# Second block of a two-block model: 32-wide products in the heads' inverse, and another order of the second input projection

## The chip, the core and the metric

The kernel runs on one core of a Trainium2 chip, as one launch. The metric is the device time in microseconds. Five engines work beside each other: PE (TensorE) multiplies matrices, with its weight loads (PEld) overlapping; DVE (VectorE), ACT (ScalarE) and POOL (GpSimd) work element by element; SP issues DMAs. They meet at semaphores only.

## The reference

Two blocks, one behind the other, on 256 tokens of 1024 channels, all in float32. The first is a mixer with a mixture of 32 experts; the second, where nearly all of the change lies, is cut here to its core:

```python
h = _rmsnorm(x, norm_mix_g)
proj = h @ w_in                       # 1024 x 7168: r, k, v | glu_in | gate logits
rkv = rkv + (_token_shift(rkv) - rkv) * mu_rkv
# low-rank products on h + dh * mu_lora[j], dh = shift(h) - h
w_log = -softplus(-(w0 + tanh(xw @ w1) @ w2)) - 0.5;  a = sigmoid(a0 + (xa @ a1) @ a2)
g = sigmoid(xg @ g1) @ g2
# per head (16 heads of 64), over 256 steps:
S = S * w_t + (S @ -kk_t) (kk_t * a_t)^T + v_t k_t^T ;  o_t = S @ r_t
o = group_norm(o) * ln_g + ln_b + bonus;  a_out = o * g
u = glu_in[:1024] * sigmoid(glu_in[1024:])      # then a causal convolution, 31 taps per channel
c_out = silu(layer_norm(conv(u)))
x = x + (gates0 * (a_out @ w_rwkv) + gates1 * (c_out @ w_conv)) @ w_out
x = x + square(relu(h2 @ w_ff1)) @ w_ff2
```

## The kernel before

The 256 tokens stand as two tiles (`NT = 2`) of 128 partitions. Dense weights come in quarters of 128x1024 by SP's DMAs into a ring of four (`RING = 4`). Each is split: ACT writes the high part `whi` (line 301), POOL or DVE the rest `wlo` (line 306), and PE does 12 products per quarter: 4 of line 326, 4 of 327, then, once `wlo` is there, 4 of 330. Each engine's order is written out by hand, function by function, and a wait names a semaphore and a count.

**The second input** (`pe_in2`, `act_in2`, `dve_in2`). 14 tiles of 512 columns, p = 0 to 13, four quarters each, in the order `TILES2`. Two PSUM banks take one tile, the next two the next, so tile p waits until tile p - 2 has been read out.

- p = 0 to 3 are the gated input of the convolution. ACT copies or sigmoids each tile out of PSUM (line 2269), and `gate_glu(j)` on DVE multiplies the halves (line 2352). PE then turns the result by transposes (`turn_u`, line 2183) and DVE copies it to `uT` (`copy_u`, line 2393).
- The low-rank products (lines 2204 and 2206, then 2218) need `lora_in` less `lora_lerp`: DVE multiplies the weights by mu (line 2382), subtracts (2385), and scales `hT` (2387).
- `convolve` on DVE is 31 rounds for each of two sets of four chunks, so 62 rounds of 4 instructions (lines 2411 and 2414), accumulating in PSUM. They are dealt out between DVE's other work by `CONV_FIRST` and `CONV_NEXT`.
- p = 4 to 9 are r, k, v. `shift_out` scales two products of each tile (lines 2330, 2335), ACT moves the result down one token by three DMAs (2281 to 2283), and `shift_in` adds (2344). PE's tile p + 2 waits for it.
- p = 10 to 13 are the gates, with a bias product of one row (line 2167) ahead of each. Behind tile 11 come `cs`, a cumulative sum for the first pair of heads (line 2232), then `pe_conv_back`, which transposes the convolution's result (line 2450) and waits for it and for `pdiff`, a DVE difference (line 2510) made from `cs`.

**The heads** (`pe_heads`, `act_heads`, `dve_heads`). 16 heads are worked as 8 pairs, p = 0 to 7, one `step` each; steps 1 to 6 are a loop, and steps 0 and 7 have parts of the dense products between their pieces. A pair is four units (2 heads, 2 token tiles), each with a triangular 128x128 matrix whose inverse is built by doubling over 7 levels. At a level, PE makes `below` (line 2672), DVE masks it (`mask`, line 3105), PE makes `grow` (lines 2686 and 2691), and ACT copies halves of it back (`grown`, lines 2918 and 2919). At levels 0 to 5 these are products of 64x64 on the two diagonal halves (`HALF`), which sit on two separate quarters of PE's array. Between `below` and `grow` PE has a piece of the pair before (`rest`, `solve`, `state`, `outputs`, products over 128 partitions) or of the next (`turn_ar`, `turn_bk`, `grams`). `begin_inverse` on DVE makes the level-0 operands: one pass (line 3089) and two masks (3093) for each two units.

**The experts.** `pe_scatter` adds a group's result to the tokens by four products (line 1743) into banks 3, 6, 7, 3; the fourth waits until DVE has added the first (line 1751).

## Time and profile before

| | |
|---|---|
| median of 3 runs | 1346.9 us (1345.45 to 1347.27) |
| the profiled execution | 1349.64 us, of it the span 1347.7 us |
| PE busy in the span | 1289.7 us (96%) |
| DVE / ACT / POOL busy | 848.8 (63%) / 724.2 (54%) / 571.8 us (42%) |
| granted TensorE clock, mean | 0.978 |

The times of all rows come from the one profiled execution, from the start of its span. The second input stands at about 682 to 929 us, the heads at 929 to 1100 us. PE's busy time is modelled from pipelined matmuls, so 96% does not say that it works at its peak: a stretch is judged by what ended the idle time and by how densely instructions start. PE does a float32 product as two instructions in the trace: a line that the code's order shows as x4 has x8 in the timeline.

### The profile page before, as it was taken

What the parts mean: (1) busy time and instruction counts of PE and PEld (TensorE: products, weight loads), DVE (VectorE), ACT (ScalarE), POOL (GpSimd) and SP (SyncE); (2) the same over time, 40 slices, a digit from 0 to 9 for tenths busy, and PEclk for the clock granted to TensorE, in tenths of its full rate; (3) what the DMA queues carried; (4) which work ended last, traced back from release to release, by engine and by line L of the source; (5) the groups of instructions that cost most, each with busy time, mean ns of one, the idle gap of its engine ahead of it and who ended that gap; (6) DMA issues with size and microseconds to landing.
All of it is one profiled execution on the core that took longest, in us unless ns stands there. A gap on an engine that the chain in (4) does not pass through costs nothing.

```text
span 1347.7 us, 22434 instructions
## 1 busy us (share of the span) xinstructions
PE 1289.7 (96%) x7929; PEld 1040.8 (77%) x7929; DVE 848.8 (63%) x1578; ACT 724.2 (54%) x1252; POOL 571.8 (42%) x252
## 2 busy tenths in 40 slices
PE   7999999897999999999999899899999999999997
PEld 6978878786887887877677677676888877788886
DVE  1576466547788888888568998854777763221213
ACT  5564666546666776766564133574433334554544
POOL 5886674350000000000489257645100017788884
PEclk9999999898899999999999898989999999999999
DMA  6665453267799999997476266633100006555552
GB/s 216 192 185 144 131 166 125 63 188 246 243 343 318 323 315 337 318 305 266 135 221 196 86 186 190 202 88 113 56 3 2 18 2 204 160 185 188 185 192 89
DMA packets 128515, 240.07 MB, mean 178 GB/s; under 512 B 16428, under 2 KB 23470, under 8 KB 128420
## 3 DMA queue, kind: packets, MB, share of 16 engines
q1 hardware_dynamic: 116656, 227.12, 52.8%
q10 hardware_dynamic: 11765, 11.67, 3.3%
q8 instruction: 62, 1.02, 0.3%
q14 instruction: 32, 0.26, 0.1%
HBM read 234.57 MB, written 1.05 MB: 175 GB/s over the span
## 4 chain that ended last, share of the span: by engine, by line
issue 44%; PE 24%; POOL 18%; DVE 10%; DMA 3%; ACT 1%; ACTq 1%; POOLq 0%; DVEq 0%
POOL wlo L306 18%; DVE bank L2414 4%; PE bank L326 3%; PE bank L330 3%; PE bank L327 3%; DMA work<-proj 2%; PE bank L2672 2%; PE bank L2686 2%; PE bank L2691 1%; PE bank L2648 1%; PE bank L2736 1%; PE bank L2716 1%; PE bank L2708 1%; PE bank L2737 0%; DVE proj L2344 0%
## 5 line engine op out<-in xcount | busy, mean ns | idle before, releaser
L306 POOL TENSOR_TENSOR wlo<-raw,whi 128x1024 fp32r<-128x1024 f32 (+1 forms) x232 | 560.9, 2437 | 619.9 <-ACT whi L301 615.4
L301 ACT ACTIVATE whi<-raw 128x1024 fp32r<-128x1024 f32 (+1 forms) x300 | 312.0, 1055 | 254.0 <-PE bank L330 130.1
L326 PE MATMUL bank<-whi,t0h 128*128 128x512 f32 (+1 forms) x552 | 226.3, 410 | 6.1 <-ACT whi L301 3.9
L327 PE MATMUL bank<-whi,t0l 128*128 128x512 f32 (+1 forms) x552 | 221.1, 401 | 0.0
L330 PE MATMUL bank<-wlo,t0h 128*128 128x512 f32 (+1 forms) x552 | 151.7, 397 | 1.6 <-POOL wlo L306 1.6
L326 PEld LDWEIGHTS bank<-whi,t0h 128*128 128x128 f32 x552 | 106.5, 193 | 37.8 <-issue 6.3
L330 PEld LDWEIGHTS bank<-wlo,t0h 128*128 128x128 f32 x552 | 105.8, 192 | 26.8 <-POOL wlo L306 2.9
L327 PEld LDWEIGHTS bank<-whi,t0l 128*128 128x128 f32 x552 | 106.6, 193 | 23.2 <-issue 1.0
L306 DVE TENSOR_TENSOR wlo<-work,whi 128x1024 fp32r<-128x1024 f32 x96 | 113.1, 1220 | 7.7 <-ACT whi L301 7.7
L1660 PE MATMUL bank<-whi,t0h 128*128 128x512 f32 x256 | 106.8, 417 | 0.0
L1661 PE MATMUL bank<-whi,t0l 128*128 128x512 f32 x256 | 102.2, 399 | 0.0
L301 ACT ACTIVATE whi<-work 128x1024 fp32r<-128x1024 f32 x96 | 98.3, 1059 | 3.7 <-PE bank L1687 3.7
L2414 DVE SCALAR_TENSOR_TENSOR bank<-work,proj,bank 128x256 f32<-128x256 f32 x232 | 96.4, 485 | 1.6
L306 DVE TENSOR_TENSOR wlo<-raw,whi 128x1024 fp32r<-128x1024 f32 x68 | 81.8, 1242 | 12.7 <-ACT whi L301 12.4
L3511 DVE TENSOR_TENSOR bank<-bank,work 128x256 f32<-128x256 f32 x32 | 13.4, 428 | 112.9 <-ACT work L3436 112.9
L1665 PE MATMUL bank<-wlo,t0h 128*128 128x512 f32 x256 | 81.8, 401 | 0.0
L3012 POOL TENSOR_TENSOR proj<-proj,small x8 | 4.9, 617 | 138.6 <-PE bank L2737 138.6
L1665 PEld LDWEIGHTS bank<-wlo,t0h 128*128 128x128 f32 x256 | 48.6, 191 | 12.8 <-DVE wlo L306 1.1
L1660 PEld LDWEIGHTS bank<-whi,t0h 128*128 128x128 f32 x256 | 49.3, 192 | 10.8 <-issue 0.7
L1661 PEld LDWEIGHTS bank<-whi,t0l 128*128 128x128 f32 x256 | 48.9, 191 | 10.7 <-issue 0.7
L2918 ACT COPY work<-bank 128x64 f32<-128x64 f32 x80 | 17.1, 214 | 68.2 <-PE bank L2691 62.4
L1761 ACT ACTIVATE t1h<-bank 128x256 fp32r<-128x256 f32 x32 | 12.4, 387 | 75.0 <-PE bank L1671 75.0
(528 smaller groups left out, 2514.2 us busy)
## 6 DMA issues: line engine op xcount, KB each, us to landing
raw<-in_w_in SPq DMA_DIRECT2D x96, 512.0 KB, 3.8
raw<-in_w_ff SPq DMA_DIRECT2D x64, 512.0 KB, 3.7
work<-in_w_exp_down SPq DMA_DIRECT2D x68, 256.0 KB, 6.0
work<-in_w_exp_gate SPq DMA_DIRECT2D x62, 256.0 KB, 5.9
work<-in_w_exp_up SPq DMA_DIRECT2D x62, 256.0 KB, 7.2
raw<-in_w_exp_down SPq DMA_DIRECT2D x60, 256.0 KB, 5.6
raw<-in_w_in SPq DMA_DIRECT2D x20, 464.0 KB, 4.2
raw<-in_w_exp_gate SPq DMA_DIRECT2D x34, 256.0 KB, 5.9
```

Source lines behind the costliest of these rows:

```text
L301: nc.scalar.activation(whi[:, s, 0:width], raw_of(n)[:, 0:width], ACT.Copy).then_inc(hi_ready, 1)
L306: ins = (nc.vector if split_by_vector(n) else nc.gpsimd).tensor_tensor(wlo[:, s, 0:width], raw_of(n)[:, 0:width], whi[:, s, 0:width].bitca ...
L326: nc.tensor.matmul(dst[t][:, 0:width], hi[:, k, r], wh[:, kk, :], start=k == 0 and not begun, stop=False)
L327: nc.tensor.matmul(dst[t][:, 0:width], lo[:, k, r], wh[:, kk, :], start=False, stop=False)
L330: mm = nc.tensor.matmul(dst[t][:, 0:width], hi[:, k, r], wl[:, kk, :], start=False, stop=k == KC - 1)
L1660: nc.tensor.matmul(dst, t0h[:, k, r], wh[:, :, kk, :], start=k == 0, stop=False)
L1661: nc.tensor.matmul(dst, t0l[:, k, r], wh[:, :, kk, :], start=False, stop=False)
L1665: mm = nc.tensor.matmul(dst, t0h[:, k, r], wl[:, :, kk, :], start=False, stop=k == KC - 1)
L2414: ins = nc.vector.scalar_tensor_tensor(out=cvT[:, c, :] if w == W2 - 1 else partial(c), in0=uT[:, c, w:w + SEQ], scalar=tap, in1=partial(c ...
L2672: mm = nc.tensor.matmul(o[r], gram[b][r, u, r], ident[r, r] if lev == 0 else Xm[r, u, :], start=True, stop=True)
L2686: nc.tensor.matmul(bank[2 + g][r, v * 64:(v + 1) * 64], XD[b][r, u, :], Ym[r, u, :], start=True, stop=True)
L2918: nc.scalar.copy(halves(Xm[:, r, :], lev)[0], halves(new[:, 0], lev)[0]).then_inc(xm_copied.sem, 1)
```

## The change

It has three parts.

1. **Inverse.** At levels 0 to 4 the blocks are at most 32 wide, so the products are made on the four diagonal 32x32 blocks (`BLOCK`, `SMALL = 5`) in place of the two 64x64 halves. Level 0 makes both operands by products with the identity, which `mask_first` masks in one pass, and the masks of line 3093 go. At level 4 ACT spreads the 32-wide result to 64 with zeros by four scaled copies for each two units in place of two copies. On DVE the preparation of the next pair is dealt out anew (`make_r`, `make_a`, `sum_bonus`, `squares`), and `centre` loses one instruction.
2. **Second input.** `TILES2` starts 8, 6, 9, 7: the sigmoid half of each gated pair comes first and the other is multiplied straight out of PSUM in `gate_glu`, so two of four evacuations go. The products by mu (`lerp`) are made by ACT. `turn_u(1)` moves inside tile 4, `cs` ahead of tile 11, `pdiff` ahead of the last six rounds of the convolution.
3. **Experts.** The fourth product of `pe_scatter` goes to bank 2, without the wait; the next block's use of bank 2 waits instead.

```diff
                     if q == 1:
+                        if added:
+                            pe.wait_ge(x_added, added)
                         turn_hidden(E, b)
...
-                if z == 3:
-                    pe.wait_ge(x_added, 4 * J - 3)
-                nc.tensor.matmul(bank[(3, 6, 7, 3)[z]][:, :], back[:, J - 1, t, :], ysum[:, 512 * h:512 * h + 512],
+                nc.tensor.matmul(bank[(3, 6, 7, 2)[z]][:, :], back[:, J - 1, t, :], ysum[:, 512 * h:512 * h + 512],
...
-        TILES2 = [6, 8, 7, 9] + list(range(6)) + list(range(10, 14))
+        TILES2 = [8, 6, 9, 7] + list(range(6)) + list(range(10, 14))
...
-        CONV_FIRST, CONV_NEXT = (12, 8, 4), (3, 2)
+        CONV_FIRST, CONV_NEXT, CONV_LAST = (10, 3, 7, 2), (3, 2), 4
-            return min(tiles, RKV2) + max(tiles - GATES2, 0)
+            return (min(tiles, RKV2) + 1) // 2 + max(tiles - GATES2, 0)
...
+                elif p in (3, 5):
+                    pe.wait_ge(*glu_ready.at(p - 1))
...
-            tile(4)
-            turn_u(1)
+            def second_chunks():
+                pe.wait_ge(*lora_act.at(3))
+                turn_u(1)
+
+            tile(4, second_chunks)
...
-            for p in range(9, 12):
-                tile(p)
-
+            tile(9)
+            tile(10)
             pe.wait_ge(*state_decay_ready.at(1))
             mm.then_inc(cs_done, 1)
+            tile(11)
...
+            def lerp(j):
+                c = (slice(0, 64), slice(64, P), slice(P, 2 * P))[j]
+                for k in range(KC):
+                    ins = nc.scalar.activation(lora_lerp[:, k, c], lora_in[:, k, c], ACT.Copy, scale=mul[:, j, k:k + 1])
+                ins.then_inc(lora_lerped, 1)
...
+            act.wait_ge(lora_in_loaded, 48)
+            lerp(0)
+            lerp(1)
...
-                if p < RKV2:
-
-                    f = slice((p // 2) * TW + (p % 2) * D, (p // 2) * TW + (p % 2) * D + TW)
+                if p < RKV2 and p % 2 == 0:
...
+                    if p == 12 and q == 1:
+                        act.wait_ge(pdiff, 1)
+                        nc.scalar.activation(FIRST[1], FIRST[1], ACT.Exp, scale=-S_DECAY).then_inc(pexp.sem, 1)
...
-                dve.wait_ge(*evac2.at(NT * (2 * j + 2)))
+                dve.wait_ge(*evac2.at(NT * (j + 1)))
+                dve.wait_ge(quarter_done, Q_IN2 + 8 * j + 8)
                 for t in range(NT):
-                    nc.vector.tensor_tensor(glu[:, t, f], glu[:, t, f], glu[:, t, g], ALU.mult).then_inc(glu_ready.sem, 1)
+                    nc.vector.scalar_tensor_tensor(out=glu[:, t, f], in0=bank[2 + t][:, :], scalar=in2_scale[:, t:t + 1],
+                                                   in1=glu[:, t, g], op0=ALU.mult, op1=ALU.mult).then_inc(glu_ready.sem, 1)
...
-            for j, c in enumerate((slice(0, 64), slice(64, P), slice(P, 2 * P))):
-                if j == 2:
-                    gate_glu(0)
-                order.mark(nc.vector.tensor_tensor(lora_lerp[:, :, c], lora_in[:, :, c],
-                                                   mul[:, j, :].unsqueeze(2).to_broadcast([P, KC, c.stop - c.start]), ALU.mult))
-            order.settle()
+            dve.wait_ge(lora_lerped, 3)
             nc.vector.tensor_tensor(lora_in, lora_in, lora_lerp, ALU.subtract).then_inc(xw_ready, 1)
+            gate_glu(0)
...
+            at = convolve(at, CONV_LAST)
+            dve.wait_ge(*pexp.at(2))
+            nc.vector.tensor_tensor(FIRST[1], bank[4][:, 0:2 * P].rearrange("p (t s) -> p t s", t=NT), decay[:, :, 0:P],
+                                    ALU.subtract).then_inc(pdiff, 1)
             convolve(at, W2 * len(CONV_SETS))
...
+        BLOCK = [slice(32 * q, 32 * q + 32) for q in range(4)]
+        SMALL = 5
+        Xs, Ys = Ym[:, :, 0:32], Xm[:, :, 0:32]
+        XDs = [XD[c][:, :, 0:32] for c in range(2)]
+        X_AND_XD = [carve(9216 + 256 * c, 2, 4, 64)[:, :, :, 0:32] for c in range(2)]
...
+                        if lev == 0:
+                            x, xd = (64, 0) if b == 0 else (0, 64)
+                            for r in BLOCK:
+                                nc.tensor.matmul(bank[g][r, x + v * 32:x + v * 32 + 32], gram[b][r, u, r], ident[r, r],
+                                                 start=True, stop=True)
+                            for r in BLOCK:
+                                mm = nc.tensor.matmul(bank[g][r, xd + v * 32:xd + v * 32 + 32], ident[r, r],
+                                                      gram[b][r, u, r], start=True, stop=True)
+                            continue
+                        if lev < SMALL:
+                            for r in BLOCK:
+                                mm = nc.tensor.matmul(bank[g][r, v * 32:v * 32 + 32], gram[b][r, u, r], Xs[r, u, :],
+                                                      start=True, stop=True)
+                            continue
...
+                    if lev < SMALL:
+                        for v in range(2):
+                            u = 2 * g + v
+                            for r in BLOCK:
+                                nc.tensor.matmul(bank[2 + g][r, v * 32:v * 32 + 32], XDs[b][r, u, :], Ys[r, u, :],
+                                                 start=True, stop=True)
+                        for v in range(2):
+                            u = 2 * g + v
+                            for r in BLOCK:
+                                mm = nc.tensor.matmul(bank[2 + g][r, 64 + v * 32:64 + v * 32 + 32], Ys[r, u, :],
+                                                      XDs[b][r, u, :], start=True, stop=True)
...
-                    if lev < LEV - 1:
+                    if lev < SMALL:
+                        new = bank[2 + g][:, 0:P].rearrange("p (a u s) -> p a u s", a=2, u=2)
+                    if lev < SMALL - 1:
+                        nc.scalar.copy(halves(Xs[:, r, :], lev)[0], halves(new[:, 0], lev)[0]).then_inc(xm_copied.sem, 1)
+                        nc.scalar.copy(halves(XDs[b][:, r, :], lev)[1], halves(new[:, 1], lev)[1]).then_inc(xt_copied, 1)
+                    elif lev < SMALL:
+                        nc.scalar.activation(Xm[:, r, 0:32], new[:, 0], ACT.Copy, scale=con("even_blocks"))
+                        nc.scalar.activation(Xm[:, r, 32:64], new[:, 0], ACT.Copy, scale=con("odd_blocks")
+                                             ).then_inc(xm_copied.sem, 1)
+                        nc.scalar.activation(XD[b][:, r, 0:32], new[:, 1], ACT.Copy, scale=con("even_blocks"))
+                        nc.scalar.activation(XD[b][:, r, 32:64], new[:, 1], ACT.Copy, scale=con("odd_blocks")
+                                             ).then_inc(xt_copied, 1)
...
                     g = slice(u - 1, u + 1)```

DVE in the second input, from its memsets to the gating of the second pair (lines 2382, 2385, 2387 of before are the products by mu, the subtraction and the scaling of `hT`; 2352 gates). Before:

```order
L2377 MEMSET work 1x256 x2
L2382 TENSOR_TENSOR proj<-work,mul 128x8x64 x2
L2352 TENSOR_TENSOR proj<-proj 128x512 x2
L2382 TENSOR_TENSOR proj<-work,mul 128x8x128
L2385 TENSOR_TENSOR work<-work,proj 128x2048
L2387 TENSOR_TENSOR proj<-proj,bank 128x2048
L2398 COPY proj<-bank 128x256
L2393 COPY work<-bank 128x2x256 x2
L2411 TENSOR_SCALAR bank<-work,proj 128x256 x4
L2414 SCALAR_TENSOR_TENSOR bank<-work,proj,bank 128x256 x44
```

Now:

```order
L2408 MEMSET work 1x256 x2
L2410 TENSOR_TENSOR work<-work,proj 128x2048
L2382 SCALAR_TENSOR_TENSOR proj<-bank,factors,proj 128x512 x2
L2413 TENSOR_TENSOR proj<-proj,bank 128x2048
L2424 COPY proj<-bank 128x256
L2419 COPY work<-bank 128x2x256 x2
L2437 TENSOR_SCALAR bank<-work,proj 128x256 x4
L2440 SCALAR_TENSOR_TENSOR bank<-work,proj,bank 128x256 x36
```

Three products by mu have left DVE, the subtraction stands ahead of the gating, and the gating reads a bank.

PE at the end of tile 4 (lines 326, 327, 330 are a quarter's products, 2183 the transposes of `turn_u(1)`, 2218 the second low-rank product). Before:

```order
L330 MATMUL bank<-wlo,t0h 128x512 x4
L2183 MATMUL bank<-const,proj 128x128 x8
L2218 MATMUL bank<-work 128x512 x2
L326 MATMUL bank<-whi,t0h 128x512
```

Now, after the second quarter of tile 4 (336, 337, 340 are the quarter's products, 2196 the transposes):

```order
L340 MATMUL bank<-wlo,t0h 128x512 x4
L2196 MATMUL bank<-const,proj 128x128 x8
L336 MATMUL bank<-whi,t0h 128x512
L337 MATMUL bank<-whi,t0l 128x512
```

The transposes now have two quarters of dense products between them and the low-rank product that waits for DVE's copy of them.

PE in the loop over the heads, from level 0 to the first half of level 1 (2672 is `below`, 2686 and 2691 `grow`; 2716, 2722, 2723, 2736, 2737 are pieces of the pair before). Before:

```order
L2672 MATMUL bank<-const,work 64x64 x4
L2716 MATMUL bank<-work 128x64 x2
L2672 MATMUL bank<-const,work 64x64 x4
L2722 MATMUL bank<-work 128x128
L2723 MATMUL bank<-proj,work 128x128
L2672 MATMUL bank<-work 64x64 x8
L2736 MATMUL bank<-work 128x64
L2737 MATMUL bank<-proj,work 128x64
L2686 MATMUL bank<-work 64x64 x4
L2691 MATMUL bank<-work 64x64 x4
```

Now (2701 and 2704 are level 0, 2709 `below`, 2731 and 2736 `grow`):

```order
L2701 MATMUL bank<-const,work 32x32 x4
L2704 MATMUL bank<-work,const 32x32 x4
L2701 MATMUL bank<-const,work 32x32 x4
L2704 MATMUL bank<-work,const 32x32 x4
L2772 MATMUL bank<-work 128x64 x2
...
L2778 MATMUL bank<-work 128x128
L2779 MATMUL bank<-proj,work 128x128
L2709 MATMUL bank<-work 32x32 x16
L2792 MATMUL bank<-work 128x64
L2793 MATMUL bank<-proj,work 128x64
L2731 MATMUL bank<-work 32x32 x8
L2736 MATMUL bank<-work 32x32 x8
```

The pieces between stand where they stood; each level of 1 to 4 has twice the products, level 0 four times.

## Rows read from the trace of the kernel before

**Rows 1.** Windows by stage: span, busy of PE, PEld, DVE, ACT, POOL, clock, DMA.

```profile
682.00:929.00 247.00, 232.84 (x968) 178.59 (x966) 197.19 (x362) 113.86 (x148) 158.28 (x64) 0.94 0.58 167
961.47:981.81 20.34, 20.25 (x342) 17.35 (x344) 15.31 (x43) 7.93 (x34) 1.35 (x2) 1.00 0.01 3
```

**Rows 2.** PE's waits, 682 to 961 us: total, times, longest.

```profile
PE bank L2218 <- DVE work L2393: 5.0, 1, 5.0
PE bank L2450 <- issue: 4.4, 1, 4.4
PE bank L2183 <- DVE proj L2352: 3.0, 1, 3.0
PE bank L2672 <- DVE work L3093: 2.6, 2, 2.2
```

**Rows 3.** Timeline of DVE ahead of the convolution: start, duration, instructions, idle before.

```profile
704.59 5.33 DVE L2382 TENSOR_TENSOR proj<-work,mul 128x512 f32<-128x512 f32 x2 [1.37 <-DMA work<-in_conv_b]
714.41 3.45 DVE L2352 TENSOR_TENSOR proj<-proj 128x512 f32<-128x512 f32 x2 [4.49 <-ACT proj L2269]
...
721.21 4.38 DVE L2385 TENSOR_TENSOR work<-work,proj 128x2048 f32<-128x2048 f32 x1
725.51 2.27 DVE L2387 TENSOR_TENSOR proj<-proj,bank 128x2048 f32<-128x2048 f32 x1
728.04 1.27 DVE L2393 COPY work<-bank 128x512 f32<-128x512 f32 x2
```

**Rows 4.** Timeline of PE in the second input.

```profile
708.22 0.69 PE L2152 MATMUL bank<-proj,const 1*128 1x256 f32 x2
714.57 0.38 PE L2190 MATMUL bank<-const,work 128*128 128x128 f32 x2
766.79 3.75 PE L2218 MATMUL bank<-work 65*128 65x512 f32 x4 [5.04 <-DVE work L2393]
783.39 1.88 PE L2218 MATMUL bank<-work 65*128 65x512 f32 x4
```

**Rows 5.** Timeline of DVE at the first shift and at the convolution's end.

```profile
773.48 1.41 DVE L2330 SCALAR_TENSOR_TENSOR proj<-bank,factors,work 128x512 f32<-128x512 f32 x2
...
868.89 1.66 DVE L2414 SCALAR_TENSOR_TENSOR work<-work,proj,bank 128x256 f32<-128x256 f32 x4
872.24 0.42 DVE L2510 TENSOR_TENSOR work<-bank,proj 128x256 f32<-128x256 f32 x1 [1.69 <-ACT work L2310]
```

**Rows 6.** Timeline of ACT: the square root ahead of `in2_scale`.

```profile
697.70 0.20 ACT L475 ACTIVATE factors<-factors 128x2 f32<-128x2 f32 x1 [2.75 <-DVE factors L508]
```

**Rows 7.** Timeline of PE in a step of the heads, level 2.

```profile
1002.09 0.68 PE L2672 MATMUL bank<-work 64*64 64x64 f32 x16
...
1003.79 0.40 PE L2691 MATMUL bank<-work 64*64 64x64 f32 x8
1004.02 0.40 PE L2686 MATMUL bank<-work 64*64 64x64 f32 x8
...
1005.18 0.68 PE L2672 MATMUL bank<-work 64*64 64x64 f32 x16
```

**Rows 8.** Timeline of PE: a stream of products of 256 columns.

```profile
735.71 3.61 PE L2204 MATMUL bank<-proj,work 128*128 128x256 f32 x16
```

**Rows 9.** DVE's waits in the loop over the heads, 962 to 1080 us.

```profile
DVE work L3105 <- PE bank L2672: 17.7, 28, 1.1
```

**Rows 10.** Timeline of ACT in the loop: the two copies of one half level.

```profile
1013.67 0.21 ACT L2918 COPY work<-bank 128x64 f32<-128x64 f32 x1 [1.84 <-PE bank L2691]
1013.77 0.22 ACT L2919 COPY work<-bank 128x64 f32<-128x64 f32 x1
```

**Rows 11.** PE's waits in the experts, 400 to 650 us.

```profile
PE bank L1743 <- DVE xres L1751: 3.7, 3, 1.2
```

**Rows 12.** Windows around stalls of PE: the granted clock is the third number from the end.

```profile
764.00:774.00 10.00, 7.21 (x13) 4.40 (x14) 9.79 (x23) 0.00 (x0) 0.46 (x1) 0.51 0.33 110
931.00:935.00 4.00, 4.00 (x22) 2.48 (x22) 1.89 (x6) 0.00 (x0) 0.00 (x0) 0.57 0.01 3
```

117 lines of the change are left out of this document (75 added, 42 removed).

## The prediction

> **What bounds the kernel now.** I read the windows by stage first, then PE's waits, then the timelines of the engines that they name.
>
> In the second input (682 to 929 us) PE is busy for 232.8 of 247 us and DVE for 197.2, at a granted clock of 0.94 [rows 1]. PE's waits say who leads: 5.0 us for the copy of the turned activations, 4.4 us ahead of the transposes back (the profile names no releaser; the convolution's last products end at 870.55 and the difference of line 2510 at 872.66, so it is DVE), 3.0 us for the gating [rows 2, 5]. All are DVE's. DVE goes without a gap over 0.3 us from 714.41 to the first shift, so the convolution's end is fixed by when it starts, 729.35, the end of the copies [rows 3]. Each stall also costs clock: the window around the first has 0.51, the lower level of 1.2 GHz, and there four low-rank products take 3.75 us instead of 1.88 [rows 4, 12].
>
> In the loop over the heads it is PE. A step is 20.34 us with PE busy for 20.25 and DVE for 15.3; DVE's masks wait for PE 28 times, 17.7 us in six steps [rows 1, 9]. How PE spends it shows in level 2: `below`, 16 instructions, starts at 1002.09; `grow` is four groups of eight, two of them at 1003.79 and 1004.02; the next `below` starts at 1005.18 [rows 7]. The two groups stand 0.23 us apart: 29 ns per instruction, or 58 ns per round of two tiles.
>
> **Part 1, the inverse: -17.6 us.** The unknown is a round of four 32-wide tiles. A stream of 16 products of 256 columns takes 3.61 us with the first one's fill in it, some 220 ns each, and one of 64 columns on one tile 58 [rows 7, 8]. The line through both is 0.84 ns per column and 4 ns, so 32 wide is an estimate of 31 to 32 ns. Levels 1 to 4 have per step and level 4 + 4 rounds of `below` (16 instructions on two tiles, now 32 on four: 8 rounds) and 16 of `grow`: 96 rounds, before and now. At level 0, 8 rounds of 58 become 16 of 32. So PE's time goes from 104 x 0.058 = 6.03 to 112 x 0.032 = 3.58 us, -2.45 us per step. The pieces between stay, and so do the gaps where PE changes tile shape.
>
> Does anything else become late? Each level's period falls from 3.09 us (1002.09 to 1005.18) to about 2.46. DVE has two masks (0.5 us, narrower now) and up to four preparations of 0.42 us, 2.2 us with their waits; the new order deals them out so that no level has over four, just inside. The four masks of line 3093 (1.2 us) and the scaling in `centre` leave DVE. ACT's copies come 0.11 us apart [rows 10]; at level 4 there are four per half and not two, +0.2 us for each half, and the transposed copy of the next pair stands behind them: +0.2 us. I take -2.2 us x 8 steps = -17.6 us; steps 0 and 7 have dense products in between and save the same rounds.
>
> Bounds: at best the full 2.45, -19.6 us. If a round costs what it costs at 64 wide, 58 ns, it is 112 x 0.058 - 6.03 = +0.47 us per step, +3.7 us. The bad end is the rival below.
>
> The Trainium skill (TensorE: Matmul & The Clock Gate, section "Measured speedup vs the span model") gives about 4 ns for each further tile running beside the first, and would allow the 32 ns. No row here has four tiles at once. The same page (section "Wait — 56ns, not 53.3ns?") says that starts never come closer than about 25 ns, however small the product. By that rule, applied to every instruction of the stream, levels 0 to 4 would take 448 x 25 ns = 11.2 us per step, 5.2 more than now, and the whole change +24 us; rows have 29 ns as the mean spacing and cannot refute it.
>
> **Part 2, the second input: -12 us.** DVE comes free at 703.2 (704.59 less the 1.37 us of waiting) [rows 3]. Then the subtraction, 4.38 us as measured beside POOL, to 707.6; it needs ACT's products by mu. ACT has 24 of them: 16 stand where it sat idle for 2.75 us [rows 6], at 0.11 us spacing 1.8 us, and 8 wider ones, some 1.4 us, behind its DMA issues, done by about 701.5. The gating needs tile 1, which ends with the spread at 708.3 [rows 4], and costs two instructions of 0.7 us, the price of the shift's reads from PSUM [rows 5]: to 709.8. The scaling of `hT`, 2.27: to 712.1. Now DVE waits for PE, which reaches line 2190 at 714.57 and goes on without its 3.0 us: copies until about 717.2. The convolution starts at 717.2, not 729.35: -12.1 us. I take off 1 us, since the subtraction now lies beside POOL's split of tile 1's last quarter, for which PE would wait.
>
> From there DVE's list is the same, plus 0.4 us for the difference, plus 0.7 us where the first shift now waits for tile 4. So the last round ends near 860.3. PE reaches the transposes back at 872.76 now, 2.2 us behind the convolution, because the difference waits for two exponentials; these are done before now. Start at 860.4: -12.4 us, of which I take 12. PE itself has lost its stalls of 3.0 and 5.0 us and the slow stretch behind the second, and is there by about 851, so it waits longer than 4.4 us and for the same thing: what PE gains beyond DVE is given back at this point. From tile 12 to the heads PE leads and the 12 us stay. Bounds: 8 (half of ACT's work or the contention with POOL eats into it) and 15 (the slow clock of that stretch also goes).
>
> **At the start of the heads: -3 us.** Step 0 waits 2.2 us for line 3093, whose instruction is gone, and the clock stands at 0.57 for the 4 us behind it [rows 2, 12]: 2.2 + about 0.8. Bounds 2 and 4.
>
> **Part 3, the experts: -2.4 us.** The fourth product waits 3.7 us in three scatters [rows 11]. The new wait stands half a block of dense products later, when DVE has long added. PE leads there, but its splits and loads run close behind, so I keep two thirds; 0 and 3.7 are the bounds.
>
> Sum: -17.6 - 12 - 3 - 2.4 = -35.0. The profiled execution took 1349.6 us and gives 1314.6; the median of the runs is 2.7 lower and gives 1311.9. I forecast 1313, its own range 1305 to 1321.
>
> **Rivals.** (a) The 32-wide round gains little: between 50 ns (112 x 0.050 = 5.6, -0.4 us per step) and 58 ns (+0.47). The other parts give -17.4: 1326 to 1333. For it: no product in the trace is below the 64-wide one. Against: time falls with the columns from 256 to 64, and nothing marks 64 as the end of it.
>
> (b) The gain of the second input is lost: PE or the shifts' DMAs lead once DVE is early, and only 4 of 12 us come: 1321. For it: tiles 5 to 9 need DVE, PE and a DMA of several us in turn. Against: no wait for the shifts stands among PE's long ones [rows 2].
>
> (c) Slower. PE hands out instructions at a fixed spacing whatever the tile, and 29 ns is this spacing, not the array's time. Place: the 240 further instructions in each step. Levels 0 to 4 have 208 instructions now (6.03 us) and 448 then, 13.0 us: +7.0 per step, +56 for eight, -17.4 elsewhere: +39, 1386. It decides for slower where the spacing is over 18 ns ((6.03 + 17.4/8)/448). For it: no longer stretch of the trace has closer starts than 29 ns. Against: the two tiles of a round start within a hundredth of a us of each other, four instructions overlap at 1002.2, and 58 fits the columns.
>
> (d) The clock falls in the heads, since PE streams fewer columns per us between its shape changes. The slow level doubles what streams: a third of the 150 us at 0.5 costs some 25 us and leaves about 1338. Against: it is 1.00 in the loop now, and fell only behind stalls.
>
> **Chances.** Forecast 0.57; (a) 0.16; (b) 0.13; (c) and the shorter spacing of the rule above 0.08; (d) 0.03; no gain that shows, because two of these meet, 0.03. The range reaches from 1303 over (a) and (b) to 1334 and leaves about 0.18 out. The runs of before spread over 1.8 us, so less than 0.2% (2.7 us) is no change. Faster: the forecast, (a), (b) and half of (d), 0.88; same 0.02; slower 0.10.
>
> **What the profile after would show.** Steps in the loop of about 18.1 us, with groups of eight 32-wide instructions some 0.065 us apart (0.1 in (a), 0.23 in (c)). The convolution's first product near 717 and its last near 860. No wait of PE at the turned activations, 6 to 9 us ahead of the transposes back, none at level 0 of step 0. Wrong if a step stays above 19.5 us, or if DVE's masks in the loop no longer wait for PE: then DVE bounds it.

## The result, and the profile after

The changed kernel takes 1335.3 us in the median of 7 runs (1330.4 to 1339.4), the kernel before 1347.3 (1345.1 to 1349.1): ratio 0.990, interval 0.9882 to 0.9918. It is faster, by 12 us and not by the 34 forecast, and just outside the range of 1303 to 1334. The profiled executions have spans of 1334.3 and 1347.7 us, so the traces hold the whole difference, 13.4 us. I cut them at five products of PE that both have:

| from .. to | before | after | moved | forecast |
|---|---|---|---|---|
| start .. last product of the experts' fourth scatter | 648.7 | 644.1 | -4.6 | -2.4 |
| .. first sums of decays of the heads | 279.4 | 269.6 | -9.8 | -12 |
| .. state of pair 0 (step 0 and the start of step 1) | 29.74 | 23.91 | -5.8 | -5.2 |
| .. state of pair 7 (seven steps) | 141.08 | 148.50 | +7.4 | -15.4 |
| .. end | 248.7 | 248.1 | -0.6 | 0 |

Ahead of the heads' loop the sum came out, 20.2 us for 19.6, in part by luck: the experts gave more than forecast and the second input less. The seven steps were to lose 15.4 us and gained 7.4: nearly the whole error is there.

Windows of the seven steps, first the kernel before, then the changed one (columns as in [rows 1]):

```profile
957.89:1098.97 141.08, 139.82 (x2347) 119.18 (x2344) 102.59 (x285) 54.25 (x228) 9.42 (x14) 1.00 0.04 13
```

```profile
937.67:1086.17 148.50, 135.93 (x3981) 113.47 (x3977) 89.71 (x254) 58.69 (x256) 9.39 (x14) 0.91 0.05 14
```

Three things are to be seen. PE has 3981 products where it had 2347. It is idle for 12.6 us where it had been idle for 1.3. And the granted clock is 0.91 where it was 1.00, so that the busy time is little smaller although the work is.

The small products themselves are as fast as forecast. PE's timeline of the changed kernel in step 3 (start, duration, instructions, idle before):

```profile
992.02 0.33 PE L2731 MATMUL bank<-work 32*32 32x32 f32 x16
992.17 0.31 PE L2736 MATMUL bank<-work 32*32 32x32 f32 x16
...
992.46 0.26 PE L2736 MATMUL bank<-work 32*32 32x32 f32 x9
993.37 0.25 PE L2736 MATMUL bank<-work 32*32 32x32 f32 x5 [0.65 <-issue]
...
996.38 0.45 PE L2718 MATMUL bank<-work 64*64 64x64 f32 x8
997.09 0.45 PE L2718 MATMUL bank<-work 64*64 64x64 f32 x8 [0.27 <-ACT work L2979]
997.98 1.13 PE L2680 MATMUL bank<-work 64*128 64x256 f32 x8 [0.43 <-ACT work L2966]
```

Sixteen 32-wide instructions start 0.15 us after the sixteen before them: 9 ns each, or 37 ns per round of four, where eight 64-wide ones took 0.23 [rows 7]. But in the middle of a group of sixteen PE stands still, with no semaphore between the two products: "issue" is the profile's word for a wait that nothing in it explains. I call such a stand a stop, and give its length from the start of the last product before it to the start of the next, which is some 0.2 us more than the idle time in the brackets. And at level 5 it now waits for ACT (lines 2979 and 2966), which it did not before.

The longest such stop, 3.2 us, is in level 1 of step 1, and the clock falls behind it. PE's timeline there, then the windows (the clock is the third number from the end, DMA's share the second):

```profile
939.56 0.31 PE L2731 MATMUL bank<-work 32*32 32x32 f32 x12
942.87 0.26 PE L2731 MATMUL bank<-work 32*32 32x32 f32 x2 [3.00 <-issue]
```

```profile
938.00:939.00 1.00, 1.00 (x39) 0.84 (x37) 0.73 (x4) 0.00 (x0) 0.00 (x0) 1.00 1.00 242
940.00:941.00 1.00, 0.00 (x0) 0.00 (x0) 0.45 (x2) 0.09 (x2) 0.00 (x0) 1.00 0.90 338
945.50:963.65 18.15, 18.12 (x373) 15.22 (x371) 9.91 (x27) 6.67 (x29) 1.34 (x2) 0.64 0.01 3
983.68:1003.63 19.95, 18.41 (x581) 15.36 (x581) 13.22 (x39) 8.46 (x37) 1.34 (x2) 1.00 0.01 3
```

Step 1 takes 27.4 us; steps 2 to 4, at full clock, 20.0, 20.0 and 19.7, where [rows 1] has 20.34 and I forecast 18.1.

Counting the products between the stops gives the first theory. Counted from 905 us they stand behind products 515, 766, 1397, 1523, 1650, 2027, 2153, 2657, 2784, 3161, 3287, 3665, 3792 and 4296: some 126 apart, or a multiple of that. With its weight load each product is two instructions, so 126 products and the few other instructions between them are about 256. The third part of the profile's page has the queue that carries PE's instructions, 16 KB in each packet (packets, MB, share); first before, then after:

```profile
q8 instruction: 62, 1.02, 0.3%
```

```profile
q8 instruction: 77, 1.26, 0.4%
```

In the trace the block for the stop at 992.5 starts to come at 991.10 and takes 0.94 us; PE goes on at 993.37, 1.3 us behind its landing. The stops end 1.2 to 1.7 us behind a landing, and no two blocks start to come closer together than 3.3 us. So theory 1: **PE gets its next 256 instructions only some 3.4 us after it began the last 256, and small products use them up sooner.** Theory 2 is my rival (d), a clock that falls because fewer columns stream. Theory 3 puts the blame on other places: the second input gave less than I read, or ACT's copies are the bound.

Second input and experts, PE's waits in the changed kernel from 655 to 915 us, and the longest one from 400 to 655:

```profile
PE bank L2481 <- DVE work L2440: 6.0, 1, 6.0
PE bank L340 <- POOL wlo L316: 3.6, 3, 2.0
```

```profile
PE bank L1693 <- ACT whi L311: 1.5, 1, 1.5
```

The wait of 5.0 us at the turned activations and the 3.0 of the gating are gone, the one at the transposes back has grown from 4.4 to 6.0 ([rows 2] against these), and that of the scatters [rows 11] is gone. The waits for POOL's split have grown from 1.4 to 3.6 us.

### The profile page after: what moved, and what is told of

It reads as the page before. It is cut to its first block, busy times and chain, and to the rows that moved or that the text cites. A ratio compares the mean times of both kernels' runs of the same rounds, so it can differ in the third digit from the quotient of the medians.

```text
span 1334.3 us, 26278 instructions
## 1 busy us (share of the span) xinstructions
PE 1274.2 (95%) x9849; PEld 1028.4 (77%) x9849; DVE 819.0 (61%) x1535; ACT 733.9 (55%) x1305; POOL 569.5 (43%) x252
## 3 DMA queue, kind: packets, MB, share of 16 engines
q10 hardware_dynamic: 11765, 11.59, 3.3%
q8 instruction: 77, 1.26, 0.4%
## 4 chain that ended last, share of the span: by engine, by line
issue 44%; PE 29%; POOL 19%; DVE 4%; ACT 1%; DMA 1%; POOLq 0%; ACTq 0%; DVEq 0%
POOL wlo L316 19%; PE bank L340 4%; PE bank L336 4%; PE bank L337 4%; DVE bank L2440 2%; DMA work<-proj 1%; PE bank L2680 1%; PE bank L2731 1%; PE bank L2709 1%; PE bank L2792 1%; PE bank L2736 1%; PE bank L2772 1%; PE bank L2764 1%; PE bank L2793 1%; PE bank L2217 1%
## 5 line engine op out<-in xcount | busy, mean ns | idle before, releaser
L316 POOL TENSOR_TENSOR wlo<-raw,whi 128x1024 fp32r<-128x1024 f32 (+1 forms) x232 | 558.4, 2425 | 601.7 <-ACT whi L311 598.2
L311 ACT ACTIVATE whi<-raw 128x1024 fp32r<-128x1024 f32 (+1 forms) x300 | 311.9, 1054 | 256.6 <-PE bank L340 136.3
L336 PE MATMUL bank<-whi,t0h 128*128 128x512 f32 (+1 forms) x552 | 225.0, 408 | 6.6 <-ACT whi L311 4.9
L337 PE MATMUL bank<-whi,t0l 128*128 128x512 f32 (+1 forms) x552 | 218.9, 397 | 0.0
L340 PE MATMUL bank<-wlo,t0h 128*128 128x512 f32 (+1 forms) x552 | 151.5, 396 | 3.6 <-POOL wlo L316 3.6
L336 PEld LDWEIGHTS bank<-whi,t0h 128*128 128x128 f32 x552 | 105.5, 191 | 36.8 <-issue 7.6
L340 PEld LDWEIGHTS bank<-wlo,t0h 128*128 128x128 f32 x552 | 105.0, 191 | 28.8 <-POOL wlo L316 4.9
L337 PEld LDWEIGHTS bank<-whi,t0l 128*128 128x128 f32 x552 | 105.6, 191 | 23.2 <-issue 1.2
L316 DVE TENSOR_TENSOR wlo<-work,whi 128x1024 fp32r<-128x1024 f32 x96 | 113.0, 1219 | 7.6 <-ACT whi L311 7.6
L311 ACT ACTIVATE whi<-work 128x1024 fp32r<-128x1024 f32 x96 | 97.7, 1053 | 3.6 <-PE bank L1697 3.6
L2440 DVE SCALAR_TENSOR_TENSOR bank<-work,proj,bank 128x256 f32<-128x256 f32 x232 | 96.4, 484 | 1.6
L316 DVE TENSOR_TENSOR wlo<-raw,whi 128x1024 fp32r<-128x1024 f32 x68 | 81.7, 1240 | 12.4 <-ACT whi L311 12.1
L3609 DVE TENSOR_TENSOR bank<-bank,work 128x256 f32<-128x256 f32 x32 | 13.3, 427 | 112.8 <-ACT work L3534 112.8
L1693 PE MATMUL bank<-whi,t1h 128*128 128x512 f32 x128 | 50.8, 397 | 1.5 <-ACT whi L311 1.5
```

The costliest lines, as they stand in the source:

```text
L311: nc.scalar.activation(whi[:, s, 0:width], raw_of(n)[:, 0:width], ACT.Copy).then_inc(hi_ready, 1)
L316: ins = (nc.vector if split_by_vector(n) else nc.gpsimd).tensor_tensor(wlo[:, s, 0:width], raw_of(n)[:, 0:width], whi[:, s, 0:width].bitca ...
L336: nc.tensor.matmul(dst[t][:, 0:width], hi[:, k, r], wh[:, kk, :], start=k == 0 and not begun, stop=False)
L337: nc.tensor.matmul(dst[t][:, 0:width], lo[:, k, r], wh[:, kk, :], start=False, stop=False)
L340: mm = nc.tensor.matmul(dst[t][:, 0:width], hi[:, k, r], wl[:, kk, :], start=False, stop=k == KC - 1)
L1693: nc.tensor.matmul(bank[4 + h][:, :], hh, whi[:, s, f], start=first, stop=False, skip_group_check=True)
```

## The experiments

Each run's median and ratio are against the kernel before, run on the same chip beside it. The medians scatter more than most of the effects: the changed kernel gave 1335.3 and, run again, 1328.8 us. What tells the theories apart is the trace, so the table has the stages of each profiled execution: from the last scatter to the heads, the seven steps, and in these PE's busy time and the clock.

| run | 32-wide levels | to the heads | seven steps | PE busy, clock | median | ratio, interval |
|---|---|---|---|---|---|---|
| before | none | 279.4 | 141.08 | 139.8, 1.00 | | |
| part1 | 0 to 4 | 276.6 | 146.19 | 132.8, 0.94 | 1349.9 | 1.0022 (1.0006 to 1.0039) |
| wide | none | 268.2 | 141.07 | 139.8, 1.00 | 1333.8 | 0.9899 (0.9873 to 0.9925) |
| changed | 0 to 4 | 269.6 | 148.50 | 135.9, 0.91 | 1335.3 | 0.9900 (0.9882 to 0.9918) |
| again | 0 to 4 | 268.9 | 147.87 | 134.1, 0.93 | 1328.8 | 0.9872 (0.9839 to 0.9905) |
| small4 | 0 to 3 | 270.2 | 146.36 | 139.2, 0.92 | 1331.2 | 0.9870 (0.9846 to 0.9894) |
| small3 | 0 to 2 | 267.3 | 145.11 | 139.4, 0.95 | 1334.2 | 0.9910 (0.9879 to 0.9941) |
| late | 0 to 4 | 266.0 | 150.42 | 136.6, 0.91 | 1334.1 | 0.9915 (0.9882 to 0.9948) |
| late2 | 0 to 4 | 271.5 | 144.11 | 131.3, 0.95 | 1332.5 | 0.9889 (0.9851 to 0.9926) |
| small3_late2 | 0 to 2 | 274.3 | 138.54 | 132.7, 1.00 | 1330.8 | 0.9869 (0.9848 to 0.9890) |
| half | 0 to 4 | 267.8 | 148.94 | 136.9, 0.90 | 1330.9 | 0.9879 (0.9861 to 0.9896) |
| best | 0 to 2 | 268.6 | 138.58 | 132.5, 1.00 | 1323.8 | 0.9828 (0.9810 to 0.9847) |

**wide: all of the change but the inverse.** The old inverse in the changed kernel:

```diff
-        SMALL = 5
+        SMALL = 0
-                            for r in BLOCK:
-                                nc.tensor.matmul(bank[g][r, x + v * 32:x + v * 32 + 32], gram[b][r, u, r], ident[r, r],
...
+                            mm = nc.tensor.matmul(o[r], gram[b][r, u, r], ident[r, r] if lev == 0 else Xm[r, u, :],
...
+                        nc.vector.tensor_tensor(XD[c][r, g, :], gram[c][r, g, r],
+                                                con("level0_t")[r].unsqueeze(1).to_broadcast([64, 2, 64]),
```

> The changed kernel with the old inverse (64-wide products at every level, level 0 masked from gram), and with everything else of the change. Theory 1 (supply): with the 32-wide products PE goes through 256 instructions, which is 16 KB, in less time than the next 16 KB of instructions take to arrive (some 3.5 us from the start of one to the use of the next), stands still, and the clock falls behind the longer stalls. Then the 64-wide form has no gap over 0.3 us inside its groups, loop steps of 20.3 us at clock 1.00, and the kernel takes what the changed one has gained ahead of the heads: 1347.3 - 16.7 = 1330 to 1331, some 4 to 5 us below the changed kernel. Theory 2 (few columns): the clock falls in the heads because the array streams less; gives the same time here, but with no claim on gaps. Theory 3 (the second input and the experts gave less than I read): 1335 or more.

Seven steps of 20.3 us, to 0.01 us those of before, no issue wait among PE's waits there, and a time like that of the changed kernel: parts 2 and 3 alone bring 12 us. The expected lead of 4 to 5 us over the changed kernel shows in no median (1333.8 against 1335.3 and 1328.8). In the traces the seven steps are 7 us shorter but step 0 is 4.4 longer (28.27 against 23.91), which I had left out: the wait of 2.2 us for DVE's level-0 masks is back in it.

**part1: the inverse alone**, on the second input and the experts of before.

```diff
-        TILES2 = [8, 6, 9, 7] + list(range(6)) + list(range(10, 14))
+        TILES2 = [6, 8, 7, 9] + list(range(6)) + list(range(10, 14))
...
-                nc.tensor.matmul(bank[(3, 6, 7, 2)[z]][:, :], back[:, J - 1, t, :], ysum[:, 512 * h:512 * h + 512],
+                nc.tensor.matmul(bank[(3, 6, 7, 3)[z]][:, :], back[:, J - 1, t, :], ysum[:, 512 * h:512 * h + 512],
```

> The kernel before with the change of the inverse alone (32x32 products at levels 0 to 4, the new order of VectorE in the heads); second input and experts as before. My prediction said -17.6 - 3: 1326. Theory 1 (supply): the work saved in the groups of products comes back as gaps at the 16 KB boundaries, one long stall in step 1 and half clock behind it: 1346.2 - 2.2 (no wait for the masks of step 0) + 2 to 4, that is 1344 to 1350, with loop steps of 19.2 to 22 us. If parts 2 and 3 give 12 to 13 us by themselves (the run with the old inverse), the sum of both must give the changed kernel's 11 to 12.

1.0022, with an interval above 1: by itself the part from which I wanted 17.6 us and the start of the heads make the kernel slower by 0.2%. The profiled execution is the fastest of its 12, 10 us below their median, at a clock of 0.980 (the others 0.960 to 0.973), and even there the seven steps are 5.1 us longer than before, with PE busy 7 us less. Its waits in them, with the stops of the supply in front:

```profile
PE bank L2714 <- issue: 5.4, 4, 2.7
PE bank L2663 <- ACT work L2949: 2.0, 5, 0.4
PE bank L2719 <- issue: 1.8, 2, 1.2
PE bank L2701 <- ACT work L2962: 1.5, 5, 0.4
```

**micro: the supply by itself.** It computes nothing of the reference, and was executed once. `small` is a stream on four 32x32 tiles and `wide` one on two 64x64 tiles, both straight code; the last line shown runs beside 16 loads of 512 KB.

```diff
+            small(768).then_inc(done, 1)
...
+            wide(768).then_inc(done, 1)
...
+            with pe.Fori(0, 12):
+                small(64)
...
+            small(768).then_inc(done, 1)
```

> Nothing of the reference: only streams of products on TensorE, with a pause between them, and zeros as the output. In order: 768 products of 32x32 on four tiles as straight code; 768 of 64x64 on two tiles as straight code; a loop of 12 rounds over 64 products of 32x32; 192 products of 256 columns; then the first two again, the first of them beside 16 loads of 512 KB. Theory 1 (supply): 128 products are 256 instructions or 16 KB, and the next 16 KB come 3.3 to 3.5 us after the start of the last. The first stream takes 6 x 3.4 = 20 us in six bursts of 1.0 us with gaps of some 2.4 us between; the second, at 29 ns each, needs 3.7 us for 128 products and runs without gaps, 22 us; the loop's body fits in one piece and, if it is kept, runs at 8 ns: 6 us; beside the loads the gaps grow. Theory 2 (nothing is supplied late, the clock only follows the columns): the first stream takes 768 x 8 ns = 6 us (12 at half clock) without regular gaps.

Each call on float32 became two products with two weight loads in the trace, so a stream has 1536 products, twice what the expected 20 us counted, and a round of the loop 256 instructions. PE's timeline in the first stream (bursts), in the loop, and beside the loads:

```profile
7.32 0.21 PE L59 MATMUL bank<-w 32*32 32x32 f32 x1 [1.86 <-issue]
...
8.94 0.30 PE L59 MATMUL bank<-w 32*32 32x32 f32 x7
11.04 0.21 PE L59 MATMUL bank<-w 32*32 32x32 f32 x1 [1.80 <-issue]
...
95.24 0.26 PE L57 MATMUL bank<-w 32*32 32x32 f32 x8 [0.15 <-issue]
...
207.90 0.26 PE L59 MATMUL bank<-w 32*32 32x32 f32 x2 [2.62 <-issue]
```

Windows of the first stream, the 64-wide one, the loop, and the small stream beside the loads and behind them:

```profile
2.25:45.00 42.75, 23.23 (x1538) 21.66 (x1540) 0.91 (x1) 0.00 (x0) 1.00 0.02 5
45.00:92.30 47.30, 47.30 (x1536) 47.30 (x1536) 0.00 (x0) 0.00 (x0) 1.00 0.02 4
93.80:110.80 17.00, 15.61 (x1538) 14.30 (x1538) 0.00 (x0) 0.00 (x0) 1.00 0.00 1
203.00:232.00 29.00, 11.59 (x768) 10.78 (x768) 0.00 (x0) 0.00 (x0) 0.50 0.66 232
232.50:247.00 14.50, 8.06 (x536) 7.53 (x540) 0.00 (x0) 0.00 (x0) 0.50 0.02 5
```

Instructions that came in 41 us of the first stream, and in 23 us beside the loads (none in the 15 us of the loop):

```profile
q8 instruction: 12, 0.20, 1.9%
```

```profile
q8 instruction: 4, 0.07, 1.1%
```

The straight small stream runs, behind a first burst of 223, in bursts of exactly 128 products, then stands still: one burst every 3.45 to 3.73 us, 41.1 us for 1536. With their weight loads 128 products are 256 instructions, so a packet of 16 KB is 256 instructions of 64 bytes. The loop does as many in 17.0 us, 8.6 ns each, since its instructions stay. The 64-wide stream needs 30.9 ns a product, 3.95 us a block, and never stops: it is just slow enough. Beside loads a block takes 4.6 to 6.7 us. Theory 2 has no place for any of this. (In the first stream a product takes 13.3 ns, as it does later at clock 0.50; the records of the clock begin only at 50.6 us, and the 1.00 of its window is no reading.)

**small4, small3: fewer small levels.** For small3 (small4 has 4 in both places):

```diff
-        if lev == 5:
-            put("level5", np.tile(np.eye(64) + pick, (2, 1)))
+        if lev >= 3:
+            put(f"level{lev}", np.tile(np.eye(64) + pick, (2, 1)))
...
-        SMALL = 5
+        SMALL = 3
```

> 32-wide products at levels 0 to 2 only, 64-wide from level 3 on: 96 fewer products per step than in the changed kernel. Theory 1 (supply): a step is 17.9 us of work plus 1.2 us for two levels at 64 wide plus at most 0.3 us of gaps: 19.1 to 19.5 us; gaps inside groups only where levels 1 and 2 meet a 16 KB boundary; 1322 to 1328. Theory 2 (few columns): the array streams more, but the drops of the clock stay in half: about 1330. Theory 3 (ACT's four copies where the shape changes): the wait of 0.8 us moves from level 5 to level 3, steps as in theory 1 plus 0.5.

> 32-wide products at levels 0 to 3, 64-wide from level 4 on: 48 fewer products per step than in the changed kernel. Theory 1 (supply): 17.9 + 0.6 us of work and gaps of 0.5 to 0.9 us per step at the 16 KB boundaries: 19.0 to 19.4 us; whether the long stall in step 1 stays depends on the 1 MB of loads there; 1323 to 1330. Theory 2: between the changed kernel and the run with three small levels, about 1332.

Half confirmed. small3's quiet steps take 19.7 us, 0.64 below 64-wide ones; over the seven steps the stops of over 0.45 us at the end of a block go from 8 (8 in the run again too) to 4 in small4 and 3 in small3. But both kernels keep a stop of 1.6 to 2.5 us in step 1, and steps 1 of 25 us with it, so the gain is not collected, and both medians lie above what was expected. PE's waits for ACT fell: 0.8 us in all seven steps for the copies of the last small level.

**late, late2: the loads of step 1.** The long stop of step 1 stood beside DMA at a share of 1.0: SP issues the broadcast row `ln_x_b` at 936.63 and a quarter of the projection at 937.00, 512 KB each, just when the next block of instructions is due (PE begins the block before it at 936.5, and elsewhere the next comes 1.1 to 1.2 us after that; here it comes at 940.66). The first added wait is in late2 alone, the second in both.

```diff
             for j, dst, name in ((1, ka_row, "k_a_2"), (2, lng, "ln_x_g_2"), (3, lnb, "ln_x_b_2")):
                 wait_low(sp, Q_RWKV + j)
+                if j == 3:
+                    sp.wait_ge(*gram_done.at(4 * 3))
                 sp.dma_start(dst, row(A[name][0], D)).then_inc(rk_loaded if j == 1 else rows_loaded, 16)
+            sp.wait_ge(*gram_done.at(4 * 5))
             rwkv(4)
```

> The changed kernel with one load of 512 KB (the fifth quarter of the projection behind the heads) issued some 45 us later: it waits for the products of gram of step 3, and so does not run behind the broadcast row ln_x_b in step 1. Nothing else changes. Theory 1 (supply): the stall of 3.2 us inside the products of level 1 in step 1 comes from the 16 KB of instructions that stood behind 1 MB of data; with half of the data it falls to about 1 us or less and the 17 us at half clock behind it go: 8 to 9 us gained, 1326 to 1328. The short gaps at the 16 KB boundaries stay (1.2 us per step). Theory 2 (few columns): clock and time as in the changed kernel, 1335.

> The changed kernel with both loads of step 1 moved out of the stretch of small products: the broadcast row ln_x_b waits for the last products of gram of step 1, the fifth quarter of the projection for those of step 3. Theory 1b (the long stall of step 1 comes from 16 KB of instructions that queue behind the 512 KB of the broadcast row): no stall over 1.3 us in step 1, the fetch there comes within 4 us of the use of the one before; step 1 takes 20 to 21 us and not 25.8 to 27.4; the kernel gains 5 to 7 us over the changed one, 1328. Theory 1c (the late fetch belongs to this place of the program, whatever the DMA queues carry): the stall of 2.4 to 3.2 us stays, 1334.

late missed: with one load moved the stop is still there, only shorter, and its clock drop as well. late2 holds it: with both moved no stop in step 1 is over 1 us and the step takes 20.8 us instead of 26 to 27.4. PE's timeline at the place, late and then late2:

```profile
938.19 0.27 PE L2732 MATMUL bank<-work 32*32 32x32 f32 x2 [2.25 <-issue]
```

```profile
941.13 0.22 PE L2734 MATMUL bank<-work 32*32 32x32 f32 x2 [0.53 <-issue]
```

So the broadcast row by itself is enough to hold the instructions up (2.4 us in late), and with the other load beside it the stop is 3.2 us; the row alone was not moved. The kernel before and wide carry the same two loads in step 1 and have no stop there: in these no block starts to come until 4.7 and 5.1 us behind the issue of the first of them (956.48 and 961.19, 940.81 and 945.88). again and half have the same stop of 3.2 us in the same group of products: it is no accident of one execution. In the medians late2 gains nothing that can be told from the scatter, where 1328 was expected.

**small3_late2: both**, with ACT's copies at the last small level dealt out anew: those that PE waits for first, for both halves, then the transposed ones.

```diff
+                if lev == SMALL - 1:
...
+                    for g in range(2):
...
+                        nc.scalar.activation(Xm[:, r, 0:32], new[:, 0], ACT.Copy, scale=con("even_blocks"))
...
+                    for r, new in views:
+                        nc.scalar.activation(XD[b][:, r, 0:32], new[:, 1], ACT.Copy, scale=con("even_blocks"))
...
```

> 32x32 products at levels 0 to 2 only, both loads moved as in the run before, and ACT's copies where the shape changes put in another order: the ones that PE waits for first, for both halves, then the transposed ones. Theory 1 (supply): steps of 19.3 to 19.8 us, no stall over 1.2 us and no drop of the clock in the heads; the heads take 7 x 0.8 = 6 us less than with the old inverse: 1325 to 1328. If the clock falls in the heads without a stall ahead of it, theory 1 is wrong on the clock.

Seven steps in 138.5 us, 10 below the changed kernel and 2.5 below 64-wide ones, at a clock of 1.00 without a drop: one stop of over 0.45 us at the end of a block is left (0.88). The order of the copies was no gain: the wait for them went, and PE waits 3.4 us in seven places for ACT at another product (of `outputs`). The median, 1330.8, is above the 1325 to 1328 expected, and cannot be told from that of wide (1333.8): what the small products of levels 0 to 2 are worth, 2.5 us, shows in the traces alone.

**half, best, again.** again is the changed kernel once more (1328.8, below the 1332 to 1336 expected). In the other two the transposes back from the convolution stand half a tile later, alone in half and with small3_late2 in best:

```diff
-            pe_conv_back(pe)
-            tile(12)
+            tile(12, lambda: pe_conv_back(pe))
```

> The changed kernel with PE's transposes back from the convolution moved half a tile later, into tile 12 of the second input. Theory A (the wait of 6 us for VectorE's convolution costs its own length and the half clock behind it, 13.7 us long in the profile): the wait goes to 0 to 1 us and the clock stays at 1.00 there; ACT's chain behind the transposes takes 11 us, so a new wait of 3 to 4 us appears ahead of the transposes of the normed convolution; 3 to 5 us gained by the start of the heads (269.7 us behind the last scatter before, 265 to 267 after). Theory B (what is late is VectorE, and the work behind it moves with it): the new wait takes all of it, nothing gained.

> Small products at levels 0 to 2, both loads moved, and the transposes back half a tile later: the sum of what the runs so far point to. By the traces the seven steps of the heads take 138.5 us (148.5 in the changed kernel), and theory A gives 3 to 5 us ahead of them: 1326 us, range 1322 to 1331. If theory B holds, 1330.

> The changed kernel itself, so that it shares the chip and the runs with the two others: 1332 to 1336. Its profile is a second sample of where the fetches of instructions fall: by theory 1 again 8 to 11 gaps of over 0.45 us at the 16 KB boundaries in the heads and one of 2 to 3 us in step 1.

half: the wait of 6.0 us is gone, and another of 4.1 us stands in its place, with the slow stretch behind it:

```profile
PE bank L407 <- ACT work L2509: 4.1, 1, 4.1
```

```profile
870.00:884.00 14.00, 12.04 (x31) 8.20 (x32) 11.83 (x11) 11.18 (x14) 9.93 (x4) 0.53 0.38 114
```

Up to the heads it takes 267.8 us, within what the other kernels scatter (266.0 to 274.3): theory B holds for most of it. best is the fastest kernel here, 0.9828, its interval wholly below that of the changed kernel and of the kernel before; against that of again the intervals overlap at their ends (0.9847 and 0.9839). Its windows of the seven steps:

```profile
935.24:1073.82 138.58, 132.47 (x3309) 111.81 (x3304) 91.10 (x254) 60.51 (x256) 9.70 (x14) 1.00 0.05 15
```

## Why the prediction was wrong

**Part 1, -17.6 us, is the step that failed.** I wrote that PE's time goes from 6.03 to 3.58 us per step and that the pieces between stay. The first half is right: from first to last start a group of `below` takes 0.26 us instead of 0.46, the `grow` of a level 0.56 for 0.93. With the change to the next shape it is 0.38 for 0.61 and 0.68 for 1.08, four times each, and 0.81 for 0.78 at level 0: 2.45 us less per step, as forecast. (By luck to the last digit: a round took 34 to 37 ns and not 32, and the steps to the next shape became shorter, which I had taken to stay.) The second half is wrong. I counted rounds of the array and gave the 240 further products and 240 further weight loads of a step a price only in a rival. What the runs show in their place, over seven steps of the changed kernel: 12.6 us idle for 1.3, of it 8.3 in the eight stops at the ends of blocks of 256 instructions and 3.5 in waits for ACT, and 27 us at the lower clock behind three of the stops. An estimate of what each cost: a step at full clock has PE busy for 18.4 us instead of 20.25, so seven would save 12.9; 3.9 were saved, so the clock took 9.0; and -12.9 + 9.0 + 11.3 of idle time is the 7.4 measured. At 1.00 in small3_late2 PE is busy 132.7 us with less of the small form, here 135.9. micro gives the law, small3_late2 and late2 show that stops and drops go when the demand or the traffic goes, part1 shows that this part alone is a loss.

**ACT's four copies** at level 4 cost more than the 0.4 us per step that I gave them: PE waits 0.27 and 0.43 us for them at level 5, four times each in steps 2 to 7 of the changed kernel, 0.7 us a step. This much of theory 3 holds: 3.5 of the 12.6 us of idle time.

**Rivals.** (a) fell: a round takes 34 to 37 ns. (c) was right about the cause, the number of instructions, and wrong about its form. No fixed spacing exists: 32 products and their weight loads go out in 0.26 us, 8.5 ns a product. That also measures the rule of the Trainium skill cited there (TensorE: Matmul & The Clock Gate, "Wait — 56ns, not 53.3ns?"), no closer than 25 ns: it does not hold with four small tiles. But 3.45 us for 128 products is 27 ns each, so over a long stream the supply gives nearly the 29 ns that 64-wide products take anyway, and the break-even of 18 ns is crossed. That the kernel escaped the 1386 us fits the sum of a step, an estimate: its 581 products are 4.6 blocks, 15.7 us at 3.45 each, less than the step takes, so only its dense stretches starve. (d) is right in that the clock fell and wrong in its reason: the drops of the changed kernel in the heads start at 941.7, 1033.8 and 1054.3, each within 4 us of the start of a stop of 1.2 to 3.2 us; in small3_late2 and best, with no stop of 0.9 us, there is none. And steps 2 to 4 of the changed kernel, 60 us with every level below 5 at 32 wide, stay at 1.00.

The Trainium skill has the mechanism, on a page that I had not weighed (Runtime: NRT & Kernel Launch, "Instruction fetch mechanics"): blocks of 16 KiB, the next one fetched while the current one runs. The traces agree with both: packets of 16 KB, and in micro the next starts to come 1.0 to 1.4 us behind the start of a burst of the first stream. The same section also says that the cost is mostly hidden, since instructions go out more slowly than they are fetched. Here they go out in 1.1 us a block (micro, the loop) and are fetched in 3.45, and nothing hides that.

**Part 2, -12 us, came to -9.8** (bounds 8 to 15). The convolution starts at 714.64, where it started at 729.35; the first line is of before:

```profile
729.35 1.89 DVE L2411 TENSOR_SCALAR bank<-work,proj 128x256 f32<-128x256 f32 x4
```

```profile
712.88 0.42 DVE L2424 COPY proj<-bank 128x256 f32<-128x256 f32 x1 [2.96 <-PE bank L2203]
713.32 1.29 DVE L2419 COPY work<-bank 128x512 f32<-128x512 f32 x2
714.64 1.89 DVE L2437 TENSOR_SCALAR bank<-work,proj 128x256 f32<-128x256 f32 x4
```

That is 14.7 us earlier, but 4.6 of them are from the experts. The 10.1 left are 2 short of the 12.1 forecast, and DVE waited for PE, as forecast: PE reached line 2203 2.5 us later than line 2190 before, counted from the last scatter, and its waits for POOL's split had grown by 2.2 us, for which I had taken off 1. The transposes back start at 857.35 (872.76 before), 10.8 us earlier without the experts, and the heads 9.8:

```profile
857.35 3.67 PE L2481 MATMUL bank<-const,work 128*128 128x128 f32 x16 [5.96 <-DVE work L2440]
```

The wait is at the low end of the 6 to 9 us forecast. The slow clock behind it is nearly all old: the kernel before had 10.3 us at 1.2 GHz behind its wait of 4.4, the changed one has 13.7. First the window of before, then that of after:

```profile
873.00:884.00 11.00, 11.00 (x31) 7.19 (x30) 7.23 (x9) 9.39 (x18) 0.00 (x0) 0.53 0.29 103
```

```profile
856.00:870.00 14.00, 12.65 (x33) 8.61 (x34) 9.12 (x15) 10.11 (x18) 0.00 (x0) 0.51 0.18 66
```

How near -9.8 is to -12 says less than it seems to: the eight executions traced here with this very code up to the heads take 266.0 to 274.3 us for the stretch, so a single trace could have said -13 or -5.

**The start of the heads, -3, and step 0's part of the inverse, -2.2, came to -5.8 together**: no wait for line 3163 is left. **Part 3, -2.4, came to -4.6**, above my upper bound of 3.7: from the first product of the scatters to the last the kernels without the new order take 222.2 and 222.7 us, those with it 217.6 to 218.1. The wait was worth more than its length: the product that waited started 1.81 us behind the one before it and not 0.43, the next 0.53 and not 0.43, so each of three scatters took 4.50 us and takes 3.00.

**Range and chances.** The sum was right to 1.2 us outside the seven steps, where the misses of part 2 and part 3 cancel, and wrong by 22.8 in them. The range could not hold this, since its upper end was (a), a case in which the array sets the pace; a case "no gain from part 1, some loss" belongs wherever a change doubles the number of instructions.

## What to carry to other kernels

Before you split products into smaller ones, count instructions, weight loads included: straight code on PE got 256 of them per 3.45 us here, some 27 ns per product, and less beside heavy loads. Below that price per product a change of shape saves nothing in a long stretch, unless the code is a loop short enough to stay, or the dense stretches are broken by large products. And price the stall behind which the clock falls, not only the stall: in this kernel one of 3.2 us cost another 4 (step 1 takes 27.4 us, the next 20.0).

## What the runs showed of the hardware

- Instructions are supplied in blocks of 256. In the heads and in micro a block of PE starts to come at least 3.3 us after the one before it, takes 0.9 to 1.5 us, and where PE stands waiting for it is used 1.2 to 1.7 us after it has landed. Beside loads at a DMA share near 1.0 it came up to 3 us late (940.66 for 937.6).
- A loop of 256 instructions fetched nothing for 15 us and cost 0.31 us per round.
- Products on four 32x32 float32 tiles start 8.5 to 8.9 ns apart at clock 1.00 (heads, and the loop of micro) and 13.3 at 0.50.
- In the seven steps of all these kernels no stop below 0.9 us was followed by a lower clock, stops of 0.9 to 1.8 us were followed by 0 to 10 us at 1.2 GHz, those of 2.4 to 3.2 us by 10 to 17. The length alone does not decide it: a stop of 2.5 us in step 0 was followed by 3.4 us at 1.2 GHz in the kernel before and by none in wide.
- Why the block of step 1 waits for the broadcast row and not for the loads of other places, and what makes the same kernel's runs differ by 10 us, stays open.
